# A hybrid decoder step on one Trainium2 core: first sample states loaded earlier, the table of turns made on GpSimd beside the retention, convolution work moved

## The chip, the cores and the metric

The kernel runs on one core of a Trainium2 chip. The metric is the device time of one execution in microseconds (us). The engines are called as the profile calls them: PE (TensorE matmul; PEld is its weight load), DVE (VectorE), ACT (ScalarE), POOL (GpSimd) and SP (SyncE, which here only issues loads). SP and POOL each issue transfers into a queue of their own; sixteen DMA engines carry them all.

## What is computed

Two layers of a decoder trunk, over 256 prompt tokens and 8 sample tokens (264 columns). In short:

```python
u = rmsnorm(h, norm_g); z = u @ w_in
s5_out, ...  = s5_branch(z[S5])          # 32 groups, 64 complex states each: scan, Re(C h) + D u, GLU
ret_out, ret_state = retention(q, k, v, g)   # 4 heads, rotary, decay, group norm, swish gate
conv_out = conv_branch(z[CONV])          # GLU, depthwise conv of width 31, layer norm, swish
merged = sum(sigmoid(gate_b) * (branch_b @ proj_b))   # three branches
h = h + merged @ w_out
h = h + (swiglu(rmsnorm(h)) if layer 0 else top-2-of-8 experts(rmsnorm(h)))
```

For each of the 8 samples the retention has a state of 4 x 128 x 256 numbers (512 KB), which is read, multiplied by the heads' decay, given the outer product of k and v, written back, and multiplied by q. All arithmetic is float32 in effect: a product of a weight block is made of three matmuls, with high and low parts of both sides.

## The kernel before, in words

Every engine has one program written out by hand; the engines meet at semaphores. The token columns are the matmuls' moving side (264 wide), with 1024 features as 8 tiles of 128.

Weights come in chunks of 8 blocks of 128 x 128 (512 KB) through a ring of 5, loaded by SP. For each chunk ACT copies the high part (L1021, `high_weights`) and DVE subtracts it (L1371, `low_weights`); PE waits for the low part. Both engines make the parts up to two chunks ahead of the tile that they are about to evict, so a DVE that waits for something else holds up the low parts, and with them PE. A tile of 8 blocks is 24 matmuls (L606 to L608), one of 4 blocks 12.

A layer's order on PE (`tile_order`): conv gates and values (cb, ca), S5 input (zs), q, k, v; then transposes (vt, kt), retention scores and outputs for four heads (sc, ou, st); transposes for the samples (vs, ks); S5 preparation (win, kk, si); then for each sample b a swish gate tile (gg), the update of the sample's state (oa, ob) and the output of the sample before (os). After that group norm (gm, gv), S5 output (y, yt), retention projections (gr, pr), S5 GLU (gl), eight pairs of S5 gate and projection (gs, ps), with the convolution's mean (cm) behind pair 3 and its variance (cv) behind pair 5, and eight pairs for the convolution (gc, pc).

The convolution's 31 taps on four feature tiles are 124 DVE operations (L1498), dealt out over the stages by the table `CONV_AT` (first number layer 0, second layer 1). The sample columns of it are `sampled_conv` (L1655), called behind merge d = 2 of the S5 projections. PE's mean waits for `conv_done`, its last operation (L1667). `conv_mean` (L1669) stands behind merge 4 and `conv_norm` (L1676) behind merge 5; the norm waits for ACT's square root of the variance, which ACT takes behind gate tile gs 6.

POOL's program for a layer: the S5 kernel preparation (powers and products), two memsets and the product `dd` of the diagonal skip; the conv state load; ten loads of S5 input (`xin`, L2002 to L2005); then it waits for the evictions of kk, adds `dd` (L2009), writes the result to the scratch `kscr` (L2011), loads states 0 and 1 (L2014), waits for the retention's `st` evictions and loads states 2 and 3 (L2018). Then come the first rows of a table of turns (powers of the S5 phase) that DVE's `sweep` uses to scan the S5 states; its later rows (`more_turns`, lines L1906 to L1915 of `product`) stand between the sample stores. For each sample b POOL waits for the updates, stores the state (L2042), for b = 1 to 4 waits for output and store of state c = b-1 and loads state c+4 into the same place (L2047), and for b < 4 issues two of eight loads of the S5 kernel table `toep` from `kscr` (L2055). PE's y products wait for all of them.

The turns and `damp` are kept in `s5m`, which also holds what the S5 preparation uses; `table` holds the rotary table, then the decay of the retention. SP reloads the rotary table for layer 1 with a weight chunk (L549).

Of the kernel before, what the change touches and what calls it, by code (L numbers as in the profile page):

```python
# [55 lines left out]
CONV_AT = {"zs": (2, 4), "v": (3, 3), "pre": (4, 4), "ret": (4, 2), "si": (16, 12), "gr": (6, 6), "gs": (3, 4)}  # L56
# [138 lines left out]
def build(nc, a):  # L195
# [16 lines left out]
    with ExitStack() as ctx:  # L212
# [78 lines left out]
        turns = s5m[:, 4096:5120].rearrange("p (r j t) -> p r j t", r=2, j=GJ)  # L291
        damp = s5m[:, 5120:5632]
# [11 lines left out]
        dd = work[0:GP, 4608:5120].rearrange("p (g q) -> p g q", g=G)  # L304
# [123 lines left out]
        conv_done = sem("conv_done")  # L428
# [17 lines left out]
        stack_zero = sem("stack_zero")  # L446
# [76 lines left out]
        def _(sp):  # L523
# [12 lines left out]
            for n in range(2, N_CHUNKS):  # L536
# [9 lines left out]
                if n == CHUNK_OF[(0, "gg", 0)] + RING:  # L546

                    sp.wait_ge(*out_of((0, "sc", HEADS - 1)))
                    sp.dma_start(rope, a["rope"]).then_inc(table_in, 16)  # L549
# [43 lines left out]
        def _(pe):  # L593
# [70 lines left out]
            for l in range(DEPTH):  # L664
# [183 lines left out]
                for d in range(KD):  # L848
                    weight_tile((l, "gs", d), "u", KD)
                    weight_tile((l, "ps", d), "g", 4)  # L850
                    if d == 3:
                        pe.wait_ge(conv_done, l + 1)
                        sum_tile((l, "cm", 0), lambda m: cT[:, m, :], 4)
# [156 lines left out]
        def _(act):  # L1010
# [52 lines left out]
            for l in range(DEPTH):  # L1063
# [39 lines left out]
                for i in range(2):  # L1103
                    key = (l, "vs", i)
                    full(key)
                    if i == 0:
                        act.wait_ge(stack_zero, l + 1)
# [48 lines left out]
                copy_out(key, os_rows, at(key)[:, 0:DV])  # L1156
                gate_of("gr", 0, 0)
# [197 lines left out]
        def _(dve):  # L1355
# [175 lines left out]
            for l in range(DEPTH):  # L1531
# [86 lines left out]
                link(dve.memset(hst[:, :, :, 0:1], 0.0))  # L1618
                for d in range(KD):
                    sweep(l, d - 2)  # L1620
                    dve.wait_ge(s_in[d % 4], 16 * (2 * l + d // 4 + 1))
# [32 lines left out]

                def sampled_conv():  # L1655

                    dve.wait_ge(conv_state_in, 16 * (l + 1))
                    dve.wait_ge(merged, 16 * l + 3)
                    prod = tmp[:, :, :].rearrange("p a t -> p (a t)")[:, 0:NS * TAPS].rearrange("p (b k) -> p b k", b=NS)
                    for m in range(4):  # L1660
                        taps = vecs[:, l * V_L + V_DWW + m * TAPS:l * V_L + V_DWW + (m + 1) * TAPS]
                        link(mul(prod, xs[:, m, :, :], taps.unsqueeze(1).broadcast_to([P, NS, TAPS])))
                        link(dve.tensor_reduce(cT[:, m, SEQ:T], prod, AX, ALU.add))
                        if m < 3:
# [53 lines left out]
                for d in range(KD):  # L1718
# [8 lines left out]
                    if d == 5:  # L1727
                        conv_norm()
# [510 lines left out]
```

## Time and profile before

| what | value |
|---|---|
| median of 3 runs | 2037.95 us (2033.95 to 2042.22) |
| the profiled execution | 2046.39 us, its span 2044.6 us |
| granted TensorE clock, mean of the profiled execution | 0.952 of full |
| busy, share of the span | PE 92%, PEld 78%, DVE 76%, ACT 58%, POOL 18% |
| DMA | 527.54 MB, mean 258 GB/s |
| layer 0 up to the end of its mixer | about 0 to 430 us |
| layer 0, dense feed-forward | about 430 to 635 us |
| layer 1, mixer | about 635 to 1010 us |
| routing and eight experts | about 1010 to 2044 us |

Times inside the execution are counted from the span's start. A row of a timeline shows the start and the time of one instruction or of several alike, its engine and line, the tile that it writes and reads, the count, and in brackets the idle time of the engine ahead of it with what ended it. Busy time of PE is that of pipelined matmuls and their modelled ends. POOL's spans are rough.

### The profile page before, as it was taken

The numbers are of one execution on the slowest core, as the hardware profiler recorded it, in microseconds if no ns is written. First come the engines' busy times: TensorE is split into PE (matmuls) and PEld (weight loads), VectorE is DVE, ScalarE is ACT, GpSimd is POOL, SyncE is SP. The second block draws the span as 40 slices with busy tenths as digits, with TensorE's granted clock in tenths as the row PEclk, the third lists the DMA queues.
The fourth block names the chain that finished last, engine by engine and source line by source line (L and its number), as shares of the span: only waits on it lengthen the run. The fifth ranks groups of instructions, "written<-read, shape, count | busy, mean of one in ns | idle before, by whom it ended". The sixth has DMA issues, their size and how long they took to land.

```text
span 2044.6 us, 31536 instructions
## 1 busy us (share of the span) xinstructions
PE 1887.1 (92%) x11832; PEld 1600.0 (78%) x11832; DVE 1552.3 (76%) x1708; ACT 1189.8 (58%) x1227; POOL 364.3 (18%) x489
## 2 busy tenths in 40 slices
PE   7876798989998986999999999999999999999995
PEld 6865597989998975899977777777777777777774
DVE  6985587855545955796568889888898888888886
ACT  5334354544444452645466777767777777777775
POOL 7985108940000114000000000000000000000000
PEclk8987799999999997999979999999999999999998
DMA  5437744435554638444649999999999999999996
GB/s 188 165 83 188 146 155 148 144 134 179 184 176 155 211 111 225 113 165 144 260 183 354 374 365 371 381 352 378 361 376 377 355 377 367 359 379 366 380 353 238
DMA packets 98098, 527.54 MB, mean 258 GB/s; under 512 B 11863, under 2 KB 13431, under 8 KB 54359
## 3 DMA queue, kind: packets, MB, share of 16 engines
q1 hardware_dynamic: 86167, 488.69, 64.5%
q0 software_dynamic: 10784, 36.50, 8.3%
q8 instruction: 64, 1.05, 0.2%
q10 hardware_dynamic: 1056, 1.08, 0.1%
q14 instruction: 27, 0.22, 0.0%
HBM read 505.69 MB, written 20.54 MB: 257 GB/s over the span
## 4 chain that ended last, share of the span: by engine, by line
PE 75%; DVE 10%; issue 6%; ACT 4%; DMA 3%; POOL 1%; DVEq 0%; ACTq 0%; SPq 0%; POOLq 0%
PE bank L606 23%; PE bank L607 23%; PE bank L608 23%; DVE ring_parts L1371 2%; DVE zone L1498 2%; DMA out_ret_s<-zone 2%; DVE s5m_parts L1838 1%; PE bank L639 1%; PE bank L962 1%; ACT zone_parts L1317 1%; PE bank L917 1%; ACT ring_parts L1021 1%; DVE tmp L1562 1%; DMA zone<-in_sret 0%; DVE zone L1394 0%
## 5 line engine op out<-in xcount | busy, mean ns | idle before, releaser
L1838 DVE TENSOR_TENSOR s5m_parts<-s5m,ring_parts 128x2048 fp32r<-128x2048 f32 x228 | 519.1, 2287 | 72.6 <-ACT ring_parts L1317 72.3
L1317 ACT ACTIVATE ring_parts<-s5m 128x2048 fp32r<-128x2048 f32 x228 | 430.9, 1915 | 83.4 <-DMA s5m<-in_experts 75.8
L1371 DVE TENSOR_TENSOR ring_parts<-ring,ring_parts 128x1024 fp32r<-128x1024 f32 x238 | 312.2, 1317 | 217.1 <-ACT ring_parts L1021 178.6
L606 PE MATMUL bank<-uT_parts,ring_parts 128*128 128x264 f32 x1312 | 387.5, 295 | 36.8 <-DVE ring_parts L1371 20.9
L607 PE MATMUL bank<-uT_hi,ring_parts 128*128 128x264 f32 x1312 | 381.5, 291 | 0.0
L608 PE MATMUL bank<-uT_hi,ring_parts 128*128 128x264 f32 x1312 | 380.2, 290 | 0.0
L606 PE MATMUL bank<-s5m_parts,work_parts 128*112 128x512 f32 x896 | 359.3, 401 | 0.1
L1021 ACT ACTIVATE ring_parts<-ring 128x1024 fp32r<-128x1024 f32 x238 | 251.0, 1056 | 155.4 <-PE bank L608 121.3
L1838 DVE TENSOR_TENSOR s5m_parts<-s5m,zone_parts 128x2048 fp32r<-128x2048 f32 x112 | 255.8, 2288 | 71.7 <-ACT zone_parts L1317 71.6
L606 PEld LDWEIGHTS bank<-uT_parts,ring_parts 128*128 128x128 f32 x1312 | 257.0, 196 | 44.5 <-issue 33.0
L607 PEld LDWEIGHTS bank<-uT_hi,ring_parts 128*128 128x128 f32 x1312 | 257.6, 196 | 0.3
L608 PEld LDWEIGHTS bank<-uT_hi,ring_parts 128*128 128x128 f32 x1312 | 255.8, 195 | 0.0
L608 PE MATMUL bank<-ring_parts,work_parts 128*112 128x512 f32 x640 | 254.2, 397 | 0.0
L607 PE MATMUL bank<-ring_parts,table_parts 128*112 128x512 f32 x640 | 253.2, 396 | 0.0
L1317 ACT ACTIVATE zone_parts<-s5m 128x2048 fp32r<-128x2048 f32 x112 | 212.5, 1914 | 32.5 <-DMA s5m<-in_experts 32.0
L606 PEld LDWEIGHTS bank<-s5m_parts,work_parts 128*112 128x112 f32 x896 | 156.7, 175 | 49.4 <-issue 0.2
L606 PE MATMUL bank<-zone_parts,ring_parts 128*128 128x264 f32 x592 | 175.7, 297 | 2.6 <-DVE zone_parts L1388 1.5
L606 PE MATMUL bank<-s5m_parts,zone_parts 128*112 128x512 f32 x448 | 177.1, 395 | 0.0
L607 PEld LDWEIGHTS bank<-ring_parts,table_parts 128*112 128x112 f32 x640 | 113.1, 177 | 36.0
L608 PEld LDWEIGHTS bank<-ring_parts,work_parts 128*112 128x112 f32 x640 | 112.1, 175 | 37.2
L606 PEld LDWEIGHTS bank<-zone_parts,ring_parts 128*128 128x128 f32 x592 | 114.9, 194 | 4.1 <-DVE zone_parts L1388 2.2
L1329 ACT ACTIVATE s5m<-bank 112x512 f32<-112x512 f32 x56 | 33.5, 598 | 141.9 <-PE bank L608 141.8
(317 smaller groups left out, 3080.7 us busy)
## 6 DMA issues: line engine op xcount, KB each, us to landing
s5m<-in_experts SPq DMA_DIRECT2D x340, 1024.0 KB, 6.4
ring<-in_weights SPq DMA_DIRECT2D x238, 512.0 KB, 3.3
work<-in_sret POOLq DMA_DIRECT2D x8, 512.0 KB, 12.3
zone<-in_sret POOLq DMA_DIRECT2D x8, 512.0 KB, 11.4
out_ret_s<-work POOLq DMA_DIRECT2D x8, 512.0 KB, 9.8
s5m<-kscr POOLq DMA_DIRECT2D x16, 256.0 KB, 11.3
out_ret_s<-zone POOLq DMA_DIRECT2D x8, 512.0 KB, 10.5
xT<-in_xT SPq DMA_DIRECT2D x1, 1056.0 KB, 5.1
```

What stands on the lines that cost most here:

```text
L606: pe.matmul(out, left[0], right[1], start=first, stop=False)
L607: pe.matmul(out, left[1], right[0], start=False, stop=False)
L608: return pe.matmul(out, left[0], right[0], start=False, stop=last)
L639: mm = pe.matmul(out[:, 0:T], ones[:, :], terms(i), start=(i == 0), stop=(i == n - 1))
L917: mm = pe.matmul(bank[1 + 2 * half][:, x * CAP:(x + 1) * CAP], utok[0:n, i, c:c + P], sel[0:n, i, :], start=(i == 0), stop=(i == 2))
L962: mm = pe.transpose(bank[b][:, x * CAP:(x + 1) * CAP], hm[0:CAP, t % 2, x * P:(x + 1) * P], ident[0:CAP, 0:CAP])
L1021: act.activation(weights_hi(c), weights(c, ring), ACT.Copy).then_inc(high_done, 1)
L1317: act.activation(high_slot(c), slot(c, s5m), ACT.Copy).then_inc(high_done, 1)
L1329: act.activation(hm[0:CAP, t % 2, :], bank[t % 2][0:CAP, :], ACT.Silu).then_inc(evicted[t % 2], 1)
L1371: dve.tensor_tensor(weights(c, ring_parts), weights(c, ring), f32(weights_hi(c)), ALU.subtract).then_inc(low_done, 1)
L1498: dve.scalar_tensor_tensor(out=cT[:, m, 0:SEQ], in0=xc[:, m, k:k + SEQ], scalar=vec(l, V_DWW, m * TAPS + k), in1=cT[:, m, 0:SEQ], op0=ALU. ...
L1838: dve.tensor_tensor(slot(c, s5m_parts), slot(c, s5m), f32(high_slot(c)), ALU.subtract).then_inc(low_done, 1)
```

## The change

- `CONV_AT`: in layer 0 the taps go from 3 to 2 for each v tile, from 4 to 0 ahead of the key transposes and from 4 to 3 for each head; a new stage `os` takes 2 for each sample (1 in layer 1). In layer 1 the stages up to the retention keep their numbers, and the S5 projections (`gs`) take 2 instead of 4 for each d below 3.
- `sampled_conv` goes from merge 2 of the S5 projections to the sample updates (in front of sample 1's), without the waits that it had there; `conv_norm` goes from behind merge 5 to behind merge 6; the mean waits for the taps alone.
- POOL loads states 0 and 1 as soon as its S5 preparation and the memsets are done, and states 2 and 3 behind the S5 input and the `st` evictions. All turns are made right behind that, in one go, in other places (`table`, `rstd`, `sq`). Only then does POOL make `dd` (in `gate`), add it and write `kscr`.
- The rotary table's reload waits for the swept states and goes with a later weight chunk; ACT waits for the addition ahead of gate tile gr 0; the memset's semaphore takes the place of `stack_zero`.

```diff
-CONV_AT = {"zs": (2, 4), "v": (3, 3), "pre": (4, 4), "ret": (4, 2), "si": (16, 12), "gr": (6, 6), "gs": (3, 4)}
+CONV_AT = {"zs": (2, 4), "v": (2, 3), "pre": (0, 4), "ret": (3, 2), "si": (16, 12), "os": (2, 1), "gr": (6, 6),
+           "gs": (3, 2)}
...
-        turns = s5m[:, 4096:5120].rearrange("p (r j t) -> p r j t", r=2, j=GJ)
-        damp = s5m[:, 5120:5632]
+        turns = table[:, :].rearrange("p (r j t) -> p r j t", r=2, j=GJ)
+        damp = rstd[:, :, :].rearrange("p a t -> p (a t)")[:, 0:GJ * NC]
+        spare = sq[:, 0:GJ * NC // 2].rearrange("p (j t) -> p j t", j=GJ)
...
-                if n == CHUNK_OF[(0, "gg", 0)] + RING:
-
-                    sp.wait_ge(*out_of((0, "sc", HEADS - 1)))
+                if n == CHUNK_OF[(0, "gl", 0)] + RING:
+
+                    sp.wait_ge(h_ready, 1)
                     sp.dma_start(rope, a["rope"]).then_inc(table_in, 16)
...
                     if d == 3:
-                        pe.wait_ge(conv_done, l + 1)
+                        pe.wait_ge(conv_step, (l + 1) * 4 * TAPS)
                         sum_tile((l, "cm", 0), lambda m: cT[:, m, :], 4)
...
+                act.wait_ge(kmat_ready, l + 1)
                 gate_of("gr", 0, 0)
...
+                def sampled_conv():
+
+                    dve.wait_ge(conv_state_in, 16 * (l + 1))
+                    prod = tmp[:, :, :].rearrange("p a t -> p (a t)")[:, 0:NS * TAPS].rearrange("p (b k) -> p b k", b=NS)
+                    for m in range(4):
+                        taps = vecs[:, l * V_L + V_DWW + m * TAPS:l * V_L + V_DWW + (m + 1) * TAPS]
+                        link(mul(prod, xs[:, m, :, :], taps.unsqueeze(1).broadcast_to([P, NS, TAPS])))
+                        link(dve.tensor_reduce(cT[:, m, SEQ:T], prod, AX, ALU.add))
+                        link(dve.tensor_scalar(cT[:, m, SEQ:T], cT[:, m, SEQ:T], vec(l, V_DWB, m), None, ALU.add))
+
                 for d in range(KD):
                     sweep(l, d - 2)
+                    conv_ops(l, "os")
+                    if d == 1:
+                        sampled_conv()
                     dve.wait_ge(s_in[d % 4], 16 * (2 * l + d // 4 + 1))
...
                     if d == 2:
                         assert conv_at[l] == 4 * TAPS
-                        sampled_conv()
                     if d == 4:
                         conv_mean()
-                    if d == 5:
+                    if d == 6:
                         conv_norm()
...
-                pool.memset(f32(vst_parts[0:STACK, :]), 0.0).then_inc(stack_zero, 1)
-                mul(dd, ident[0:GP, 0:GP].unsqueeze(1).broadcast_to(few), dskip[:, l, :].unsqueeze(2).broadcast_to(few)
-                    ).then_inc(gb_ready, 1)
+                pool.memset(f32(vst_parts[0:STACK, :]), 0.0).then_inc(gb_ready, 1)
+                for b in range(2):
+                    pool.dma_start(states[b], a["sret"][l, b].rearrange("h d v -> d h v")).then_inc(s_in[b], 16)
...
-                for i in range(2):
-                    pool.wait_ge(*out_of((l, "kk", i)))
-                pool.wait_ge(gb_ready, l + 1)
-                pool.tensor_tensor(toep[0:GP, :, 0:GP], toep[0:GP, :, 0:GP], dd, ALU.add).then_inc(kmat_ready, 1)
-                pool.wait_ge(kmat_ready, l + 1)
-                pool.dma_start(kscr.rearrange("g p x -> p g x")[:, :, P:2 * P], toep[0:GP, :, :]).then_inc(kscr_out, 16)
-
-                for b in range(2):
-                    pool.dma_start(states[b], a["sret"][l, b].rearrange("h d v -> d h v")).then_inc(s_in[b], 16)
...
                     pool.wait_ge(phase_ready, 2)
-                    pool.wait_ge(mm_done, DONE[(l, "si", 3)])
+                    pool.wait_ge(*out_of((l, "sc", HEADS - 1)))
...
                 first_turns()
-                more_turns(1)
-                more_turns(2)
+                for n in (1, 2, 4, 8, 16):
+                    more_turns(n)
+                pool.tensor_copy(spare[:, 0:1, 0:1], damp[:, 0:1].unsqueeze(2)).then_inc(turns_ready, 1)
+                for i in range(2):
+                    pool.wait_ge(*out_of((l, "kk", i)))
+                link(mul(dd, ident[0:GP, 0:GP].unsqueeze(1).broadcast_to(few), dskip[:, l, :].unsqueeze(2).broadcast_to(few)))
+                pool.tensor_tensor(toep[0:GP, :, 0:GP], toep[0:GP, :, 0:GP], dd, ALU.add).then_inc(kmat_ready, 1)
+                pool.wait_ge(kmat_ready, l + 1)
+                pool.dma_start(kscr.rearrange("g p x -> p g x")[:, :, P:2 * P], toep[0:GP, :, :]).then_inc(kscr_out, 16)
+
                 pool.wait_ge(kscr_out, 16 * (l + 1))
...
-                    if b < 3:
-                        more_turns(4 << b)
-                    if b == 2:
-                        pool.tensor_copy(cross[:, 0:1, 0:1], damp[:, 0:1].unsqueeze(2)).then_inc(turns_ready, 1)
```

## Rows read from the trace of the kernel before

**Rows 1.** Windows: busy us (and instructions) of each engine, clock, DMA share, GB/s.

```profile
158.00:176.00 18.00, 6.95 (x54) 6.40 (x53) 8.63 (x21) 7.41 (x13) 11.99 (x22) 0.73 0.69 202
196.00:232.00 36.00, 18.28 (x101) 14.28 (x102) 20.63 (x35) 5.29 (x8) 10.22 (x16) 0.61 0.90 218
640.00:720.00 80.00, 79.12 (x639) 78.96 (x640) 65.14 (x117) 37.43 (x54) 6.23 (x10) 0.97 0.61 188
752.00:766.00 14.00, 7.39 (x61) 6.75 (x58) 4.96 (x14) 8.07 (x14) 9.03 (x22) 0.92 0.73 214
786.00:816.00 30.00, 14.44 (x92) 11.71 (x92) 19.48 (x33) 3.40 (x5) 8.02 (x13) 0.70 0.91 240
```

**Rows 2.** Timeline of PE, layer 0: start, us, instruction, idle before it and its end.

```profile
132.04 0.79 PE L699 MATMUL bank<-zone 128*128 128x256 f32 x1 [10.03 <-DVE s5m L1578]
331.56 3.01 PE L639 MATMUL bank<-zone,ones 128*128 128x264 f32 x6 [4.38 <-DVE zone L1667]
358.93 0.59 PE L606 MATMUL bank<-uT_parts,ring_parts 128*128 128x264 f32 x1 [5.78 <-DVE ring_parts L1371]
```

**Rows 3.** Timeline of PE, layer 1, the same two places.

```profile
915.51 3.89 PE L639 MATMUL bank<-zone,ones 128*128 128x264 f32 x8 [3.82 <-DVE zone L1667]
940.54 0.39 PE L606 MATMUL bank<-uT_parts,ring_parts 128*128 128x264 f32 x1 [3.81 <-DVE ring_parts L1371]
```

**Rows 4.** Windows over a variance (layer 0) and a mean (layer 1), columns as in Rows 1.

```profile
345.20:347.40 2.20, 2.12 (x10) 1.86 (x11) 1.20 (x1) 2.19 (x4) 2.12 (x4) 1.00 0.58 203
915.40:919.40 4.00, 3.89 (x9) 3.07 (x10) 3.10 (x5) 0.00 (x0) 0.00 (x0) 0.50 0.00 0
```

**Rows 5.** Timeline of ACT, layer 0, behind gate tile gs 6.

```profile
350.26 0.39 ACT L1153 ACTIVATE gate<-bank 128x264 f32<-128x264 f32 x1 [2.87 <-PE bank L608]
352.35 1.99 ACT L1021 ACTIVATE ring_parts<-ring 128x1024 fp32r<-128x1024 f32 x2
```

**Rows 6.** Timeline of DVE, layer 0, the norm and the low parts behind it.

```profile
352.45 1.81 DVE L1680 RECIPROCAL rstd<-bank 128x264 f32<-128x264 f32 x1 [3.73 <-ACT bank L1061]
354.30 3.00 DVE L1391 TENSOR_TENSOR zone<-zone,rstd 128x264 f32<-128x264 f32 x4
357.22 3.24 DVE L1371 TENSOR_TENSOR ring_parts<-ring,ring_parts 128x1024 fp32r<-128x1024 f32 x2
```

**Rows 7.** Timeline of DVE, layer 1, the norm's four multiplications.

```profile
937.88 1.47 DVE L1391 TENSOR_TENSOR zone<-zone,rstd 128x264 f32<-128x264 f32 x4
```

**Rows 8.** Timeline of DVE, layer 0: two runs of taps; the last sample's weight part.

```profile
124.21 6.58 DVE L1498 SCALAR_TENSOR_TENSOR zone<-zone,vecs 128x256 f32<-128x256 f32 x7
154.72 6.42 DVE L1498 SCALAR_TENSOR_TENSOR zone<-zone,vecs 128x256 f32<-128x256 f32 x16
226.29 1.23 DVE L1371 TENSOR_TENSOR ring_parts<-ring,ring_parts 128x1024 fp32r<-128x1024 f32 x1 [2.69 <-issue]
```

**Rows 9.** Timeline of POOL, layer 0: input load, addition, first turn, first store, last turn.

```profile
143.81 0.64 POOL L2005 DMA_DIRECT2D s5m<-zscr  x1
158.26 4.24 POOL L2009 TENSOR_TENSOR s5m<-s5m,work 16x512 f32<-16x512 f32 x1 [13.82 <-issue]
166.44 0.49 POOL L2025 COPY s5m<-lw 128x16 f32<-128x16 f32 x2
176.98 0.78 POOL L2042 DMA_DIRECT2D out_ret_s<-work  x1 [5.30 <-DVE work L1628]
196.41 0.19 POOL L2051 COPY s5m<-s5m 128x1 f32<-128x1 f32 x1
```

**Rows 10.** Timeline of POOL, layer 1: the addition and the first store.

```profile
752.93 1.29 POOL L2009 TENSOR_TENSOR s5m<-s5m,work 16x512 f32<-16x512 f32 x1 [63.13 <-issue]
766.60 0.80 POOL L2042 DMA_DIRECT2D out_ret_s<-work  x1 [3.20 <-DVE work L1628]
```

**Rows 11.** DMA issues, 162 to 163.2 us: queue, count, KB each, us to landing.

```profile
kscr<-s5m POOLq DMA_DIRECT2D x1, 256.0 KB, 4.7
```

**Rows 12.** Timeline of ACT, layer 1: the last eviction of the retention states.

```profile
740.10 0.38 ACT L1039 ACTIVATE zone<-bank 128x256 f32<-128x256 f32 x1 [0.27 <-PE bank L718]
```

More of the change, by code:

```diff
@@ L303, in build @@
         pt1 = work[:, 2304:4608]
-        dd = work[0:GP, 4608:5120].rearrange("p (g q) -> p g q", g=G)
+        dd = gate[0:GP, :, :].rearrange("p a t -> p (a t)")[:, 0:G * GP].rearrange("p (g q) -> p g q", g=G)
         utok = work[:, 0:3072].rearrange("p (i x) -> p i x", i=3)
@@ L427, in build @@
         conv_step = sem("conv_step")
-        conv_done = sem("conv_done")
         conv_state_in = sem("conv_state_in")
@@ L445, in build @@
         pick_ready = sem("pick_ready")
-        stack_zero = sem("stack_zero")
         stack_high = sem("stack_high")
@@ L1106, in _ @@
                     if i == 0:
-                        act.wait_ge(stack_zero, l + 1)
+                        act.wait_ge(gb_ready, l + 1)
                     for lo in (64, 0):
@@ L1653, in _ @@
                     low((l, "r", m), vT[:, m, :])
[L1655 to L1664, printed above, removed]
-                            link(dve.tensor_scalar(cT[:, m, SEQ:T], cT[:, m, SEQ:T], vec(l, V_DWB, m), None, ALU.add))
-                    dve.wait_ge(conv_step, (l + 1) * 4 * TAPS)
-                    dve.tensor_scalar(cT[:, 3, SEQ:T], cT[:, 3, SEQ:T], vec(l, V_DWB, 3), None, ALU.add).then_inc(conv_done, 1)
                 def conv_mean():
@@ L2032, in more_turns @@
                     product([turns[:, r, :, n:2 * n] for r in range(2)], [turns[:, r, :, 0:n] for r in range(2)],
-                            [turns[:, r, :, n - 1:n].broadcast_to([P, GJ, n]) for r in range(2)], cross[:, :, 0:n])
+                            [turns[:, r, :, n - 1:n].broadcast_to([P, GJ, n]) for r in range(2)], spare[:, :, 0:n])
                 first_turns()
-                more_turns(1)
-                more_turns(2)
+                for n in (1, 2, 4, 8, 16):
[7 more added lines that the diff above has]
+                pool.dma_start(kscr.rearrange("g p x -> p g x")[:, :, P:2 * P], toep[0:GP, :, :]).then_inc(kscr_out, 16)
                 pool.wait_ge(kscr_out, 16 * (l + 1))
```

## The prediction

> **What bounds the kernel now.** I read the busy time by stage first [rows 1]. In most stages TensorE (PE) leaves little idle; the projections of layer 1, 640 to 720 us, are the pattern: 79.12 of 80 us busy. The sample part of the retention is the exception. In layer 0 PE is idle for 11.1 of the 18 us from 158 on and for 17.7 of the 36 us from 196 on; in layer 1 for 6.6 of 14 and 15.6 of 30. In the second stretch of each layer the DMA engines are 0.90 and 0.91 busy, so there the bound is the transfers and not an instruction. The PE timeline by what ended each gap [rows 2, 3] gives three other places: 10.03 us ahead of the retention scores of layer 0, and two waits in the S5 projections of each layer. One is for the sampled convolution (L1667): 4.38 and 3.82 us. The other is for a low weight part (L1371): 5.78 and 3.81 us.
>
> **Part 1, convolution norm (both layers).** The sampled convolution leaves the merge of d = 2, so the mean's matmuls start as soon as the taps are done: the waits of 4.38 and 3.82 go. [...] The mean's eight matmuls took 3.89 us [rows 3] where eight at full clock fit in 2.1 [rows 4]; with the rest of the next tile at half clock I take 2.6 us a layer back (between 1.8 for the eight alone and 4).
>
> The wait of 5.78 (3.81) was DVE sitting in the norm until ScalarE's root was done, with the next low weight part queued behind it. The norm now stands behind tile d = 6 and its merge, so that low part goes first. What is late next is the low part after that, which gate tile gc 1 needs. From the end of gs 6, PE has ps 6, gs 7, ps 7 and gc 0 in hand: 12+24+12+24 = 72 matmuls at 79.12/639 = 0.124 us [rows 1], 8.9 us. Against it stand, in layer 0: ScalarE from the end of the tile to its first weight copy done, 350.2 to 353.35 [rows 5], 3.2; then DVE's low part 3.24/2 = 1.6, the merge some 0.9 (estimate), the norm 1.81+3.00, and another low part 1.6 [rows 6]: 12.1 us. So a new wait of about 3.1 appears. In layer 1 the same four multiplications take 1.47 instead of 3.00 [rows 7], because POOL is quiet; I take 1 us (0 to 3).
>
> Sum: layer 0, 4.38+5.78+2.6−3.1 = 9.7; layer 1, 3.82+3.81+2.6−1 = 9.2; together 18.9. If the new wait is twice as long and the clock gives back 1.8, it is 13; without a new wait and with 4 each, 26.
>
> The sampled convolution itself (13 small operations, some 5 us of DVE) and the convolution taps that move with it (16 in layer 0, 8 in layer 1) go between the sample updates. There DVE waits for transfers (20.63 of 36 us busy [rows 1]), so I cost them nothing. If that cover were gone they cost 5+16×0.40 = 11 us in layer 0.
>
> **Part 2, taps out of the projections (layer 0).** Twelve taps leave the stretch ahead of the retention: eight in the v loop and four at the end. There POOL is busy beside DVE and seven taps take 6.58 us, 0.94 each; in the later run sixteen take 6.42, 0.40 each [rows 8]. The scores start 12×0.9 = 10.8 us earlier, the size of the wait of 10.03 [rows 2]. But this doesn't reach the end: what counts there is when POOL can start the chain of transfers, part 3. In layer 1 four taps only change places.
>
> **Part 3, states and table of turns.** The load of states 0 to 3 no longer ends last. Each following state c+4 still needs state c's update written out first, and these writes and loads share POOL's queue with the eight slices of the kernel table (toep). POOL issues the first write only when the table written to kscr has landed; in the change, the addition that feeds kscr stands behind all the turns. So the time of the first write decides, and it is worked out here.
>
> The turns are 35 POOL instructions from 166.44 to 196.41 in the trace, with the stores and loads between them [rows 9]; their own times add up to 16.2 us.
>
> Layer 0: POOL is free after its last input load (143.81+0.64, less the product of the diagonal, which moves away: about 1.1, estimated by the addition of the same shape, 1.29 [rows 10]), plus four state loads at 0.78 us as the store [rows 9]: 146.4. The DVE phases that it needs are done by about 144.7 (estimate: the retention 10 us earlier). Then 16.2 us of turns. Beside them DVE runs 16 taps, and there the addition of row 158.26 took 4.24 us against 1.29 alone in layer 1 [rows 9, 10]: it waited until the run of taps was over [rows 8]. I add 4.7 for the turns (0 to 10; 4.7 is the run of 6.42 less what is over when they start). Then product 1.1, addition 2 (1.3 to 4.24), issue 0.3, landing 4.7 [rows 11]: 146.4+16.2+4.7+8.1 = 175.4, against a first write at 176.98 [rows 9]: 1.6 us earlier (between 7 earlier and 6 later).
>
> Layer 1: nothing before the retention changes. The last state eviction ends at 740.48 [rows 12]; two state loads 1.5; turns 16.2+4.7; then 8.1: 771.0, against 766.60 [rows 10]: 4.4 us later (1 earlier to 12 later).
>
> From the first write to the last state in, 176.98 to 226.29 [rows 9, 8], is 49.3 us with the DMA engines full; bytes and order stay. POOL no longer multiplies between the transfers and PE has about one weight chunk more behind it: I take 2 us off in each layer (0 to 4). Net of part 3: 1.6−4.4+4 = +1.2 us gained.
>
> The removed wait for state 0 (11.1 and 6.6 us) is thus almost worth nothing by itself: the chain behind it starts when it started before. The moved rope load makes SP wait, with the weight loads behind it, for the swept states; they are done right after the last state is in, and the weight chunk that it goes with is due some 60 us later (estimate): nothing. ScalarE's added wait ahead of gate gr 0 is for the addition, long past: nothing.
>
> **Sum.** 18.9+1.2 = 20.1 us. The profiled execution took 2046.39 us and would become 2026.3; the runs' median is 2037.95, 8.4 below it, and 2037.95−20.1 = 2018.
>
> **Rivals.** (a) *The state wait counts in full.* If turns and kscr run early enough, 11.1+6.6 us are gained beside part 1: 2037.95−18.9−17.7 = 2001. For it: these are PE's own idle times [rows 1]. Against: the DMA engines at 0.9 right behind them.
>
> (b) *DVE becomes the bound behind the merges*: the norm delays the low parts further and half of part 1 is lost, 2037.95−9.5−1.2 = 2027. For it: DVE's weight parts at 1.6 us beside POOL [rows 6].
>
> (c) [...] The rows show one POOL addition stopped for a whole run of taps [rows 9, 8]. If each of the 35 turns instead waits for one tap, 35×0.40 = 14 us come in place of my 4.7 in each layer: 2018+2×9.3 = 2037. [...]
>
> (d) *Slower.* POOL's turns hold the kscr write in both layers by the ratio of that addition, 4.24/1.29 = 3.3. Then 16.2 becomes 53, 32 more than I took in each layer: 2018+64 = 2082. It is slower than before from a factor of 1.9 on (turns over 31 us, 20.1/2 more than mine), and by more than 0.5% from 2.2. Against it: DVE's run of taps lasts 6.4 us and its later work waits for transfers.
>
> **How the numbers follow.** Forecast 0.57, (a) 0.14, (b) 0.13, (c) 0.10, (d) 0.06. A measurement of this kernel can tell about 0.5%, 10.2 us, from no change. Faster by more is below 2027.8: nearly all of the forecast, (a), half of (b): 0.77. Within 0.5%: half of (b), (c), the end of the forecast: 0.17. Slower: 0.06. Part 1 spans 13 to 26, part 3 −18 to +16, and the outer ends of both are unlikely together; up to the nearer half of (a) and past (b) the range is 2005 to 2031.
>
> **What would show it.** No PE gap on L1667 in either layer, and the stretch of the mean at clock 1.00. A new short PE gap on L1371 at tile gc 1 in layer 0. The retention scores of layer 0 near 121 us, but si waiting for its inputs. State 0 updated some 10 us earlier in layer 0, and POOL's first write near 175 in layer 0, and late by a few us in layer 1. Wrong if the first write moves over 8 us either way, if the gap from it to the last state in differs from 49 by over 5, or if the mean still waits.

## The result, and the profile after

The changed kernel takes 2009.01 us, the median of four runs (2008.09 to 2009.79), beside 2038.59 for the kernel before in the same four rounds (2033.95 to 2042.22). The ratio is 0.9856, with a 95% interval from 0.9835 to 0.9877: 29.4 us faster (25 to 34). The forecast was 20 us, 2018, in a range from 2005 to 2031. The profiled execution of after took 2008.42 us with a span of 2006.6, close to its median. That of before lay 7.8 us above its own, so the two traces are 38.0 us apart, 8.4 more than the medians.

Where these 38 us come from is read by putting the same landmarks of both traces side by side (us from the span's start):

| landmark | before | after | shift |
|---|---|---|---|
| retention scores, layer 0 (PE L699) | 132.04 | 121.55 | −10.5 |
| first state store, layer 0 (POOL) | 176.98 | 172.55 | −4.4 |
| last weight part ahead of the last state update, layer 0 (DVE) | 226.29 | 209.07 | −17.2 |
| first convolution projection, layer 0 (PE) | 371.42 | 341.85 | −29.6 |
| root of the feed-forward's norm (ACT) | 431.51 | 399.83 | −31.7 |
| last state eviction of the retention, layer 1 (ACT) | 740.10 | 714.57 | −25.5 |
| first state store, layer 1 (POOL) | 766.60 | 741.54 | −25.1 |
| last weight part ahead of the last state update, layer 1 | 812.69 | 784.77 | −27.9 |
| experts start | 1028.7 | 990.6 | −38.1 |
| end | 2044.6 | 2006.6 | −38.0 |

So 17.2 us came up to the last state update of layer 0, 12.4 in the S5 projections of layer 0, 2.1 in its convolution projections, 2.4 and 10.2 in the chain and the projections of layer 1. 6.2 were lost between the norm of layer 0's feed-forward and the retention of layer 1. The page, first of before, then of after, has PE busy for 13.0 us less with the same 11832 matmuls, and the mean granted clock at 0.965 in place of 0.952. So of the 38 us 25 are idle time of PE, and 13 are busy time:

```profile
PE 1887.1 (92%) x11832; PEld 1600.0 (78%) x11832; DVE 1552.3 (76%) x1708; ACT 1189.8 (58%) x1227; POOL 364.3 (18%) x489
```

```profile
span 2006.6 us, 31540 instructions
PE 1874.1 (93%) x11832; PEld 1588.2 (79%) x11832; DVE 1555.5 (78%) x1708; ACT 1190.4 (59%) x1227; POOL 365.5 (18%) x489
```

The PE timeline of after at the places of [rows 2, 3], first layer 0, then layer 1:

```profile
121.55 1.22 PE L699 MATMUL bank<-zone 128*128 128x256 f32 x2 [3.43 <-DVE s5m L1579]
151.33 5.56 PE L761 MATMUL bank<-s5m 128*64 128x48 f32 x128 [7.37 <-DMA s5m<-zscr]
308.03 1.94 PE L639 MATMUL bank<-zone,ones 128*128 128x264 f32 x8
336.23 0.56 PE L606 MATMUL bank<-uT_parts,ring_parts 128*128 128x264 f32 x1 [3.73 <-DVE ring_parts L1372]
407.45 0.56 PE L606 MATMUL bank<-uT_parts,ring_parts 128*128 128x264 f32 x1 [6.88 <-DVE uT_parts L1389]
...
884.85 1.94 PE L639 MATMUL bank<-zone,ones 128*128 128x264 f32 x8
910.30 0.36 PE L606 MATMUL bank<-uT_parts,ring_parts 128*128 128x264 f32 x1 [1.04 <-DVE ring_parts L1372]
```

The convolution's mean (L639) has no bracket any more, so it doesn't wait, and its eight matmuls take 1.94 us where [rows 3] has 3.89. In place of the waits of 5.78 and 3.81 us stand 3.73 and 1.04, at gate tile gc 1. The scores start earlier, but the S5 preparation (L761) now waits 7.37 us for its input. At 407.45 is a wait of which the prediction has nothing: 6.88 us ahead of the feed-forward, for the normalised input, where the kernel before waits 4.67.

The granted clock at the two means, from windows with the columns of [rows 1], is 1.00, where [rows 4] shows 0.50:

```profile
307.80:310.20 2.40, 2.40 (x16) 2.14 (x15) 2.19 (x4) 1.06 (x1) 2.15 (x5) 1.00 0.41 131
884.60:887.00 2.40, 2.40 (x16) 2.14 (x15) 1.65 (x3) 1.06 (x1) 0.00 (x0) 1.00 0.43 142
```

The timeline of POOL in layer 0, the lines that answer to [rows 9], and behind the dots the first store of layer 1, which answers to [rows 10]:

```profile
146.77 0.93 POOL L2015 COPY table<-lw 128x16 f32<-128x16 f32 x2
150.15 0.32 POOL L1905 TENSOR_TENSOR table<-table 128x16 f32<-128x16 f32 x1
162.66 0.80 POOL L1914 TENSOR_TENSOR table<-table,sq 128x256 f32<-128x256 f32 x1
163.75 2.04 POOL L1905 TENSOR_TENSOR gate<-ident,dskip 16x512 f32<-16x512 f32 x1
165.86 1.25 POOL L2032 TENSOR_TENSOR s5m<-s5m,gate 16x512 f32<-16x512 f32 x1
167.53 0.69 POOL L2034 DMA_DIRECT2D kscr<-s5m  x1 [0.42 <-POOL s5m L2032]
172.55 0.79 POOL L2040 DMA_DIRECT2D out_ret_s<-work  x1 [4.33 <-DMA kscr<-s5m]
...
741.54 0.80 POOL L2040 DMA_DIRECT2D out_ret_s<-work  x1 [4.31 <-DMA kscr<-s5m]
```

The turns run one behind the other from 146.77 to 163.7, 16.9 us, and the first store waits for the landing in kscr, as it was put in the prediction. And DVE's lines for [rows 8], the taps beside the turns and the end of the chain of state transfers, with that of layer 1:

```profile
145.57 6.77 DVE L1499 SCALAR_TENSOR_TENSOR zone<-zone,vecs 128x256 f32<-128x256 f32 x16
209.07 1.22 DVE L1372 TENSOR_TENSOR ring_parts<-ring,ring_parts 128x1024 fp32r<-128x1024 f32 x1
784.77 1.22 DVE L1372 TENSOR_TENSOR ring_parts<-ring,ring_parts 128x1024 fp32r<-128x1024 f32 x1 [1.30 <-DMA zone<-in_sret]
```

From the first store to this point ("the chain" below) it is now 36.5 us in layer 0 and 43.2 in layer 1, where it was 49.3 and 46.1. The 36.5 are partly the luck of this execution, as the section on the chain shows.

### The profile page after: what moved, and what is told of

Same layout as the page of the kernel before. It is cut to its first block, busy times and chain, and to the rows that moved or that the text cites. A ratio compares the mean times of both kernels' runs of the same rounds, so it can differ in the third digit from the quotient of the medians.

```text
span 2006.6 us, 31540 instructions
## 1 busy us (share of the span) xinstructions
PE 1874.1 (93%) x11832; PEld 1588.2 (79%) x11832; DVE 1555.5 (78%) x1708; ACT 1190.4 (59%) x1227; POOL 365.5 (18%) x489
## 4 chain that ended last, share of the span: by engine, by line
PE 76%; DVE 11%; issue 4%; DMA 4%; ACT 4%; POOL 0%; DVEq 0%; ACTq 0%; SPq 0%; POOLq 0%
PE bank L606 23%; PE bank L607 23%; PE bank L608 23%; DVE ring_parts L1372 2%; DMA out_ret_s<-zone 1%; DVE s5m_parts L1837 1%; DVE zone L1499 1%; DMA zone<-in_sret 1%; PE bank L962 1%; PE bank L639 1%; ACT zone_parts L1318 1%; PE bank L917 1%; DMA s5m<-in_experts 1%; DVE tmp L1563 1%; DVE uT L1479 0%
## 5 line engine op out<-in xcount | busy, mean ns | idle before, releaser
L606 PEld LDWEIGHTS bank<-uT_parts,ring_parts 128*128 128x128 f32 x1312 | 255.6, 195 | 41.2 <-issue 36.5
L606 PEld LDWEIGHTS bank<-s5m_parts,work_parts 128*112 128x112 f32 x896 | 156.7, 175 | 49.3 <-issue 0.2
L1330 ACT ACTIVATE s5m<-bank 112x512 f32<-112x512 f32 x56 | 33.4, 597 | 148.1 <-PE bank L608 148.1
L1499 DVE SCALAR_TENSOR_TENSOR zone<-zone,vecs 128x256 f32<-128x256 f32 x240 | 115.8, 542 | 0.4
```

What stands on the lines that cost most here:

```text
L606: pe.matmul(out, left[0], right[1], start=first, stop=False)
L1330: act.activation(hm[0:CAP, t % 2, :], bank[t % 2][0:CAP, :], ACT.Silu).then_inc(evicted[t % 2], 1)
L1499: dve.scalar_tensor_tensor(out=cT[:, m, 0:SEQ], in0=xc[:, m, k:k + SEQ], scalar=vec(l, V_DWW, m * TAPS + k), in1=cT[:, m, 0:SEQ], op0=ALU. ...
```

## The experiments

Three questions: what is each part worth by itself, what takes back the 6 us ahead of layer 1, and why did the chain of transfers get so much shorter? The kernels of one group ran side by side on one chip. A time in us is the ratio's distance from 1 times the median of before in that group; differences of two such times carry an uncertainty of some 5 to 7 us, so a verdict on one rests on a trace line as well.

### The parts one by one

**Part 1 alone, on the kernel before**: the sampled convolution goes from behind merge 2 to the sample updates, the norm from behind merge 5 to behind merge 6.

```diff
+                    if d == 1:
+                        sampled_conv()
...
-                        sampled_conv()
...
-                    if d == 5:
+                    if d == 6:
                         conv_norm()
```

> The kernel before with part 1 alone: the sampled convolution in front of sample 1's update, the norm behind merge 6, nothing else. By the steps on record the S5 projections of the two layers give 18.9 us (13 to 26): about 2019.7 against 2038.6. If DVE becomes the bound behind the merges, half: 2029. A third theory, from the profile after: layer 1's S5 preparation on POOL, which ended 0.4 us ahead of the feed-forward's norm, now runs into it and takes back 4 to 6 us: a gain of 13 to 15, 2024 to 2025, and a first feed-forward matmul that waits about 7 us instead of 4.7.

Measured: 2029.54 us beside 2040.34, ratio 0.9944 [0.9924, 0.9964], 11.4 us faster. The mean doesn't wait, as forecast, and the wait at gc 1 is 3.8 us (forecast 3.1), but the wait ahead of the feed-forward has grown from 4.67 us to 6.34.

```profile
423.19 0.56 PE L605 MATMUL bank<-uT_parts,ring_parts 128*128 128x264 f32 x1 [6.34 <-DVE uT_parts L1387]
```

**The changed kernel without part 1** (the same edit undone).

> The changed kernel with part 1 undone: the sampled convolution again behind merge 2 of the S5 projections and the norm behind merge 5; taps, states and turns stay as changed. If the parts add up, it loses what part 1 alone gives the kernel before: about 2028 with 18.9, about 2023 if the POOL overlap at the feed-forward's norm takes 5 of it back (then that norm's PE wait is 4.7 again, not 6.9). If the states and turns were worth only the 1.2 us on record, it would be within 2 us of the kernel before, 2037.

Measured: 2023.53, ratio 0.9905 [0.988, 0.993], 19.4 us faster than before. So parts 2 and 3, for which the forecast had 1.2 us, carry two thirds of the gain, and 11.4+19.4 = 30.8 is nearly the 29.4 of the whole: the parts add up. In its trace layer 0's chain ends at 212.01, where two traces of the kernel before have 226.29 and 225.69, and layer 1's chain takes 40.2 us, where they have 46.1 and 44.6: some 14 and 5 us, which is the 19.

**The changed kernel with the old deal of the taps** (part 2 undone).

```diff
-CONV_AT = {"zs": (2, 4), "v": (2, 3), "pre": (0, 4), "ret": (3, 2), "si": (16, 12), "os": (2, 1), "gr": (6, 6),
-           "gs": (3, 2)}
+CONV_AT = {"zs": (2, 4), "v": (3, 3), "pre": (4, 4), "ret": (4, 2), "si": (16, 12), "os": (0, 0), "gr": (6, 6),
+           "gs": (3, 4)}
```

> The changed kernel with the table of taps of the kernel before (nothing between the sample updates): parts 1 and 3 stay. The prediction held that the earlier retention does not reach the end, that is 0 to 2 us slower than the changed kernel, 2009 to 2011. The rival: the turns wait for DVE's phases, which stand behind the retention; 10.5 us later they start near 155 instead of 146.8, the first state store of layer 0 comes near 181 instead of 172.6, and the time is 8 us longer, 2017.

Measured: 2021.86, ratio 0.9893 [0.9866, 0.9919], 21.9 us faster than before and about 7.5 slower than the changed kernel, little more than the uncertainty. The timeline of POOL shows how:

```profile
155.17 0.80 POOL L2015 COPY table<-lw 128x16 f32<-128x16 f32 x2 [6.92 <-DVE lw L1392]
182.06 0.79 POOL L2040 DMA_DIRECT2D out_ret_s<-work  x1 [4.24 <-DMA kscr<-s5m]
```

POOL waits 6.92 us for the phases (`lw`), which DVE makes behind the retention; the retention is back at its old time (scores at 132.16), the turns start at 155.17 in place of 146.77, and the first store goes out 9.5 us later. The twelve taps are what lets the turns start in time. The prediction said that the taps don't reach the end by themselves, but it used the earlier phases in part 3's start time; the two are one step, and apart they show it.

### The loss ahead of layer 1

**POOL's preparation for layer 1 held back.** POOL begins layer 1's S5 preparation as soon as DVE has released a tile of layer 0 (311.23 in the trace of before, 292.27 in that of after) and needs some 124 us, up to 434.7 and 416.9. The root of the feed-forward's norm is taken at 431.51 and 399.83. So the preparation's end moved by 18 us and the norm by 31.7, and in the changed kernel the norm lies wholly beside the last 17 us of the preparation. The edit makes the preparation wait until the norm is done. It then ends at 537.7, still over 150 us ahead of its use.

```diff
+                if l > 0:
+                    pool.wait_ge(u_ready, 2 * KD * l)
                 link(pool.memset(pa[:, 0, 0, :], 1.0))
```

> The changed kernel in which POOL's S5 preparation for layer 1 waits for the norm ahead of the feed-forward of layer 0 (all eight tiles written). It then runs beside the feed-forward, where DVE is half idle, and not beside the S5 and convolution projections. If POOL beside DVE is what slows DVE there (low parts 1.67 against 1.23, the norm's tiles 1.02 against 0.43), the wait of the first feed-forward matmul falls from 6.9 to about 4.7, two short ones go, and the waits behind the convolution norm in layer 0 (3.7 us) shrink to about layer 1's 1.0: 6 to 9 us, about 2001. If the slower DVE operations are hidden, 2009; if the feed-forward is slowed by it instead, up to 2015.

Measured: 1999.70, ratio 0.9799 [0.9781, 0.9817]; the changed kernel has 0.9856 [0.9835, 0.9877], so it is 11 to 12 us faster than that. The timelines of DVE and PE at the norm, first of the changed kernel, then with the preparation held:

```profile
403.45 2.90 DVE L1479 SCALAR_TENSOR_TENSOR uT<-xT,vecs,rstd 128x264 f32<-128x264 f32 x3
406.28 1.02 DVE L1389 TENSOR_TENSOR uT_parts<-uT,uT_hi 128x264 fp32r<-128x264 f32 x1
```

```profile
402.48 1.30 DVE L1479 SCALAR_TENSOR_TENSOR uT<-xT,vecs,rstd 128x264 f32<-128x264 f32 x3
403.70 0.42 DVE L1389 TENSOR_TENSOR uT_parts<-uT,uT_hi 128x264 fp32r<-128x264 f32 x1
404.27 0.56 PE L606 MATMUL bank<-uT_parts,ring_parts 128*128 128x264 f32 x1 [4.67 <-DVE uT_parts L1389]
```

Beside the preparation three norm operations take 2.90 us and a low part 1.02; without it they take 1.30 and 0.42, and PE's wait is again the 4.67 us of the kernel before. The low part at gc 1 also comes sooner: its wait fell from 3.73 to 1.0 us. What POOL does beside the norm in the changed kernel are groups like this one, with operations of some 0.8 us each:

```profile
397.03 6.29 POOL L1920 TENSOR_TENSOR work<-work 128x288 f32<-128x288 f32 x8
```

The waits aren't all of the 6.2 us: 6.88 in place of 4.67 and two new ones of 0.79 and 0.86 behind it make 3.9. The rest, some 2 us, goes with PE's clock. In the 10 us from the first feed-forward matmul on, the granted clock was 0.70 in the kernel before, 0.50 behind the longer waits of the changed kernel, and 0.75 with the preparation held, and PE had 59, 28 and 62 matmuls in them:

```profile
436.93:446.93 10.00, 10.00 (x59) 9.88 (x59) 7.16 (x15) 6.63 (x10) 0.00 (x0) 0.70 0.16 54
407.45:417.45 10.00, 8.01 (x28) 6.47 (x29) 9.32 (x13) 4.87 (x9) 9.79 (x15) 0.50 0.00 0
404.27:414.27 10.00, 10.00 (x62) 9.90 (x63) 7.40 (x16) 6.75 (x10) 5.56 (x16) 0.75 0.21 59
```

Nor is the norm the only place. Between the end of layer 0's chain and the norm, DVE's 209 instructions took 138.14 us in the changed kernel, and 208 took 123.78 with the preparation held:

```profile
209.07:378.65 169.58, 159.32 (x1338) 151.10 (x1339) 138.14 (x209) 90.98 (x147) 87.90 (x107) 0.96 0.53 155
214.55:377.68 163.13, 157.20 (x1338) 149.46 (x1339) 123.78 (x208) 90.50 (x147) 7.26 (x8) 0.97 0.56 158
```

**The same wait on the kernel before, and with part 1 alone.** This asks whether the preparation costs the same wherever it lies, or whether part 1 moved the norm into it. A third kernel splits part 1: the kernel before with only the norm behind merge 6 (`if d == 5` becomes `if d == 6`).

> The kernel before, with GpSimd's S5 preparation of layer 1 held until the feed-forward's normalised input is made. In the kernel before the preparation ends about when the mixer of layer 0 ends, so its neighbour is the S5 and convolution projections and not the norm. Theory (the preparation costs only where the norm of the feed-forward falls into it): 0 to 4 us faster, 2037 to 2041 beside a before of 2041; the wait of about 4.7 us ahead of the feed-forward stays. Rival (the preparation costs the same wherever it lies): 9 us faster, 2032, as in the changed kernel.

> The kernel before with part 1 alone, and GpSimd's S5 preparation of layer 1 held until the feed-forward's normalised input is made. Theory (part 1 is worth what was predicted, 18.9 us, and the preparation takes back what is missing): 19 us faster than before and 8 faster than part 1 alone, 2021 to 2023; no wait over 5 us ahead of the feed-forward. Rival (part 1 is worth 10.8 and the preparation is a separate 2 to 4 us): 2026 to 2028.

> The kernel before with the convolution norm behind merge 6 instead of merge 5 and nothing else: the mean of the convolution keeps its place and its wait (4.4 us in layer 0, 3.8 in layer 1). Part 1 is so split in two. Theory of the prediction: the norm gives 5.78+3.81 less a new wait of 3.1+1, so 5.5 of the 18.9 us; with the loss that GpSimd's late preparation brings, some 3 to 5 us faster than before, 2035 to 2038. Rival: the norm behind merge 6 is all of part 1's 10.8 us, and the mean's wait is made up elsewhere: 2029.

The last two columns are stretches of layer 0's traces: from the end of the chain to PE's first matmul of the feed-forward's norm, and from there to its first of layer 1's norm.

| kernel | ratio to before | us faster | waits of PE in layer 0: mean, low part, feed-forward | chain to norm | norm to norm |
|---|---|---|---|---|---|
| before (two traces) | 1 | 0 | 4.4, 5.8, 4.7 (first trace) | 184.1, 181.5 | 173.2, 173.8 |
| before, preparation held | 0.9967 [0.9954, 0.9979] | 6.7 | 3.0, 4.9 (three waits), 4.7 | 171.7 | 172.2 |
| part 1 alone | 0.9944 [0.9924, 0.9964] | 11.4 | none, 3.8, 8.0 (three waits) | 171.6 | 178.4 |
| part 1 alone, preparation held | 0.989 [0.987, 0.9911] | 22.4 | none, 1.0, 4.7 | 162.8 | 173.0 |
| norm behind merge 6 only | 0.9981 [0.9959, 1.0003] | 3.9 | 3.9, 3.3, 5.4 (two waits) | 178.3 | 173.9 |

For the kernel before, 6.7 us is more than the 0 to 4 of the first guess; its interval, 4.3 to 9.4, just reaches the 9 of the second. So the preparation costs something among the projections too. With part 1 holding it back gives 11.0 us, so part 1 is worth 22.4−6.7 = 15.7 us where POOL is quiet, and 11.4 where it isn't. The difference of 4.3 us is within the uncertainty, but it can be found in the waits: holding the preparation back takes 2.8+3.3 = 6.1 us of them away with part 1, and 1.4+0.9 = 2.3 without it, 3.8 less.

The stretches settle where. From norm to norm the five traces with part 1 and a free preparation (part 1 alone, the changed kernel, the old deal of the taps, and two kernels of the next section) took 178.4 to 179.3 us, the nine others 172.2 to 173.9: some 6 us are lost there, and only with part 1. From the chain to the norm holding the preparation back gave 10 to 12 us without part 1 and 6 to 9 with it. So part 1 didn't make the whole loss: the preparation cost time among the projections already, and part 1 brought the norm beside it as well.

The norm's half of part 1 measured 3.9 us, with an interval that takes in 0; the forecast's terms for it, 5.78−3.1 and 3.81−1, give 5.5.

### The chain of transfers

**The kernel before once more, for the spread of the chain.**

> The kernel before, unchanged, for another profile: from the first state store of layer 0 to the last state's weight part it took 49.3 us, in the changed kernel 36.5, in layer 1 46.1 and 43.2. If the transfers' rate differs from execution to execution, layer 0 shows another length here (40 to 45) and the whole is as much shorter than 2046; if the length belongs to the kernel, 49 +-1.5 again.

Its chain took 50.8 us in layer 0 and 44.6 in layer 1, against 49.3 and 46.1 in the profile shown first, so a single trace tells it to within 2 us or so in this kernel. Of the changed kernel the spread is larger: the kernel with the preparation held runs the same program up to the end of layer 0's chain, and has 44.1 us there against 36.5, and the end at 214.55 in place of 209.07. So of the 17.2 us in the table of landmarks some 5 belong to that one execution.

**The turns back between the stores**, with everything else of the change kept.

```diff
-                for n in (1, 2, 4, 8, 16):
+                for n in (1, 2):
                     more_turns(n)
...
+                    if b < 3:
+                        more_turns(4 << b)
```

> The changed kernel with the turns n = 4, 8 and 16 (24 of the 35 operations and 6 more, some 11 us) back between the state stores, as in the kernel before; the first two steps stay ahead of kscr. Then kscr is written earlier (turns end near 152 in layer 0 instead of 163.7, the first store near 166 with DVE's update of state 0) and the multiplications stand between the transfers again. If the length of the chain of stores and loads does not depend on them (49 us on record, less 2), the time is 5 to 8 us below the changed kernel: 2001 to 2004. If they are what stretched the chain in the kernel before (49.3 against 36.5 us in layer 0), the earlier start is given back: 2009 to 2020, with a chain of 42 to 49 us.

Measured: 2007.16, ratio 0.9831 [0.9807, 0.9855], the same as the changed kernel within the error. The first stores go out 9.7 and 7.2 us earlier (162.89 and 734.35), the chains take 44.4 and 47.9 us, and their ends, 207.29 and 782.26, are within 3 us of those in the profile of the changed kernel. So the new place of the turns shows no gain beside the earlier states and the earlier phases.

**Half of that: the last step of the turns (n = 16) behind the issue of the kscr write**, so that it runs while the write lands.

```diff
-                for n in (1, 2, 4, 8, 16):
+                for n in (1, 2, 4, 8):
                     more_turns(n)
...
                 pool.dma_start(kscr.rearrange("g p x -> p g x")[:, :, P:2 * P], toep[0:GP, :, :]).then_inc(kscr_out, 16)
+                more_turns(16)
```

> The changed kernel with only the last step of the turns (n = 16, six operations, 4.5 us) moved behind the issue of the kscr write, while that write is on its way (4.6 us). First store: layer 0 from 172.6 to about 167.5, layer 1 from 741.5 to about 738.5, where DVE's update of state 0 bounds it. If the first store starts the chain, 5+3 us less: 2001. If the chain's end is set by DMA work that is there anyway, no change: 2009.

Measured: 2005.86, ratio 0.9834 [0.9811, 0.9857]; against the changed kernel's 0.9856 that is within the error. The first store of layer 0 went out at 169.71, 2.8 us earlier, and the chain behind it took 44.6 us. With the preparation held as well:

> Both edits, the last step of the turns beside the kscr write and the late preparation of layer 1. If they add: 2009 less 8 less 7, about 1994. If neither counts: 2009.

Measured: 1995.18, ratio 0.9779 [0.9756, 0.9802], 45.1 us faster than before.

The chains of the kernels so far, each from one execution, fall into two groups and one case between:

| turns | kernels | chain, layer 0 | chain, layer 1 |
|---|---|---|---|
| between the transfers, states late | before (two traces), part 1 alone, norm alone, the two with preparation held | 45.9 to 50.8, mean 48.1 | 43.9 to 46.9, mean 45.6 |
| ahead, states early | changed, without part 1, old taps, last step behind the issue, the two with preparation held | 36.5 to 44.6, mean 42.2 | 39.8 to 44.4, mean 41.7 |
| between the transfers, states early | turns back | 44.4 | 47.9 |

By the means the chain is 6.0 and 3.9 us shorter, where the prediction took 2 for each layer and named 4 as the end. The 36.5 are the shortest of six; the other five have 43.3 on average.

**What is left of the chain: six of the eight table loads behind the last state load.** The S5 output starts some 17 us behind the last state, so the table has time. Both edits of the run before are kept.

```diff
-                    if b < 4:
-                        for s in (2 * b, 2 * b + 1):
+                    if b in (0, 4):
+                        for s in ((0, 1) if b == 0 else range(2, 8)):
```

> The changed kernel with the two edits of the run before (last turns behind the issue of the scratch write; preparation held), and beside them six of the eight loads of the S5 kernel table behind the load of state 7 instead of between the state transfers. Theory (from the first store to the last state in, the stretch is bound by the bytes in GpSimd's queue): 1.5 MB at 255 GB/s, some 6 us, leave the stretch of each layer, which goes from 41 to 44 us to 36 to 38; the S5 output starts some 17 us behind the last state and needn't wait for the table; 10 to 12 us faster than the run before, 1983 to 1986. Rival (bound by the round trip of one state, stored and then loaded into the same place): the stretch keeps its 41 to 44 us, 1993 to 1996, or slower where the S5 output waits for the table.

Measured: 1981.86 us, ratio 0.9731 [0.971, 0.9752]: 54.8 us faster than before, 9.7 faster than the run before it. The DMA view of layer 0's chain, first without, then with this edit (packets, megabytes, mean rate), and windows over the chains of both layers with it:

```profile
DMA packets 2976, 10.67 MB, mean 240 GB/s; under 512 B 378, under 2 KB 378, under 8 KB 2973
```

```profile
DMA packets 2329, 8.46 MB, mean 253 GB/s; under 512 B 267, under 2 KB 267, under 8 KB 2328
...
169.40:202.79 33.39, 28.07 (x224) 23.94 (x220) 32.54 (x64) 11.65 (x17) 13.41 (x19) 0.93 0.96 253
721.01:752.69 31.68, 28.60 (x224) 24.49 (x220) 30.16 (x57) 11.66 (x17) 13.39 (x19) 0.90 0.93 264
```

The chains fell from 44.5 and 41.3 to 33.4 and 31.7 us, more than the 6 expected for each. 2.2 MB fewer are moved within the chain of layer 0 (the six loads are 1.6 of them), at a rate that is hardly another. So a state's round trip isn't a fixed length, as the rival had it: the states' stores and loads took 7.1 to 11.8 us from issue to landing in the run before (medians of each kind), and 5.6 to 7.5 with the table's loads out of the way. But 1.6 MB at 240 GB/s are 6.6 us, not 11.1 and 9.6, so the bytes don't explain it all; whether the rest is the table's small rows or the order in the queue isn't shown. PE is now busy for 28.1 of the 33.4 us. The S5 output starts without a wait, at 220.62. This is the fastest version that was run.

## Why the prediction was right, and where it wasn't

The time lay in the range and 9 us below the forecast, and the sign was right. That the sum was near was luck, for two misses of opposite sign met in it: part 1 was put at 18.9 us and gave 11.4, parts 2 and 3 were put at 1.2 and gave 18 to 19.4.

**Part 1.** Each term that was read from a wait of PE held. The mean's waits of 4.38 and 3.82 us are gone, and its clock is 1.00. The 2.6 us a layer for the clock were an estimate; from the mean's first matmul to the end of the 24 of the tile behind it the traces have 7.46 and 7.33 us before and 4.67 in both layers after, 2.8 and 2.7 less. The new wait at gc 1, worked out as 3.1 and 1 us, is 3.73 and 1.04. In the traces the stretch of the S5 projections lost 12.4 and 10.2 us (forecast 9.7 and 9.2). What failed is the step "what is late next", which was followed for one tile and not to the end of the mixer. An earlier norm doesn't only move PE: the engine off the critical path, POOL with a preparation of 125 us, keeps its length, so a mixer that ends earlier meets the end of it: the norm that stands beside it costs some 6 us, 3.9 in waits and the rest beside the lower clock (0.50 in place of 0.70 in the 10 us behind the first wait). With POOL held back part 1 gives 15.7 us, inside the forecast's 13 to 26; without, 11.4.

**Part 2.** The scores came at 121.55, for "near 121", and si waits for its inputs, both as said. That it reaches the end only through POOL is borne out by the timeline of the old deal of taps.

**Part 3, the first stores.** For layer 0 the forecast was 175.4, and it is 172.55. The term that was mis-sized is the 4.7 us by which the taps were to hold up the turns: from the first to the last these took 16.9 us in layer 0 and 16.4 in layer 1, against 16.2 for their four stretches in the kernel before. (The prediction calls 16.2 the sum of their own times; it has the short pauses between them in it. The 35 instructions alone are 13.8 there, and 14.4 and 13.8 now.) In layer 1, measured from the last state eviction, the first store stands at 741.54−714.57 = 27.0 us, where it was 26.5 [rows 10, 12] and the forecast had 4.4 more than that. So the first stores came 2.9 and some 4 us ahead of the forecast.

**Part 3, the chain.** The sentence "49.3 us with the DMA engines full; bytes and order stay" failed, as the prediction's own criterion for it says (36.5, and the mean of 42.2 too, differ from 49 by over 5). The mean busy share of the DMA engines, 0.90 and 0.91 [rows 1], was taken for a bound that only the bytes move. But a share of 0.95 stood for 219 GB/s in layer 0's chain of before, and one of 1.00 for 273 in that of after; in the fastest kernel's it was 0.96 and 253:

```profile
176.98:226.29 49.31, 32.88 (x224) 27.43 (x220) 23.21 (x41) 11.64 (x17) 23.28 (x38) 0.74 0.95 219
```

```profile
172.55:209.07 36.52, 25.63 (x192) 21.49 (x192) 28.38 (x52) 9.70 (x14) 13.50 (x19) 0.86 1.00 273
```

The states and eight slices of the table share one queue. It goes faster with all four first states loaded early (the last two are issued 27.3 us ahead of the first store, at 145.25; before it was 12.0 us) and with no turns between the issues. Which of the two matters more isn't settled: the turns back between the stores lengthen the chain (44.4 and 47.9 us), but from an earlier start and to the same end. Nor is it settled why two executions of the same program up to there differ by 7.6 us.

**The rivals.** (a) put the state wait at its full 17.7 us. The amount is about right, since parts 2 and 3 gave 18 to 19.4, but the mechanism isn't that one: in layer 0 the first state update starts at 164.80 in place of 174.79 and PE's wait for it falls from 11.40 us to 2.34, but 7.37 us now stand ahead of the S5 preparation, and the first store is only 4.4 us earlier. The rest comes from the chain. With part 1 at 18.9 it would have been 2001. (b) half of part 1 lost: 7.5 of 18.9 was, but mostly through the feed-forward's norm (some 6 us), and less through the low parts behind the merges. (c) and (d), turns stretched by DVE: not by so much. DVE's sixteen taps took 6.77 us beside the turns, 0.42 each, against 0.40 [rows 8]. Of layer 0's six turns of 128x16, all beside taps, the first took 0.47 us and the others 0.32 to 0.34, where the three ahead of layer 1's taps took 0.22 to 0.24; with a tap of 0.40 to wait out, as in (c), each would have come to some 0.62. That DVE and POOL do slow each other the norm shows: beside POOL's operations of 0.8 us its low part took 1.02 us in place of 0.42. Through what, these runs don't show.

## What to carry to other kernels

When a stage is made shorter, look for the engine whose program is long and off the path, and see what it will lie on then: here a preparation that had ended with the stage took back some 4 to 6 of 16 us, and one wait in its program gave 11. A high DMA share, here 0.95 to 1.00, doesn't say that the transfers' time is fixed: ask which of them the waiting engine needs, and issue the others behind. And where one edit makes another's inputs early, cost them as one, and test them apart.

## What the runs showed of the hardware

- The busy share of the DMA engines says little of the rate. In one chain, at a share of 0.9 to 1.0 in nearly each slice, the rate went from 79 to 407 GB/s (the DMA view of the last run, layer 0, in forty slices of 0.83 us):

```profile
DMA  0395998999799999899999999998999999999999
GB/s 0 142 348 162 231 128 79 123 79 118 137 407 407 329 329 290 226 383 388 280 353 383 388 393 339 353 216 275 378 363 393 368 147 133 137 157 142 216 226 191
```

- Here a wait of PE cost more than its length. Ahead of the feed-forward the waits grew by 3.9 us, the stretch from norm to norm by 6.1 (173.2 to 179.3), and the granted clock of the 10 us behind the first wait was 0.50 in place of 0.70.
- Where DVE and POOL ran side by side, the loss differed; so did the instructions on both sides, and no single cause is isolated. Beside operations of 128x288 DVE's low part of 128x264 took 1.02 us in place of 0.42; beside copies and turns of 128x16 and 128x32 and one copy of 128x512, a tap of 128x256 took 0.42 in place of 0.40. POOL's own addition of 16x512, which took 4.24 us beside a run of taps [rows 9], took 1.25 behind it.
